# Expert stage: one row of the next turn placed ahead of a turn's ten products on the matrix engine

## The reference

```python
def peer_ffn(x, wq, subkeys, u_tab, v_tab):
    ...
        g = jax.nn.softmax(fv, axis=-1)
        a = jax.nn.gelu(jnp.einsum('thkd,td->thk', u_tab[e], xb))
        return jnp.einsum('thk,thkd->td', (g * a).astype(v_tab.dtype), v_tab[e])
...
    f = peer_ffn(x1, pwq, psk, pu, pv)
    e = jax.nn.sigmoid(x1 @ wpg) * (p @ wpp)
    return layer_norm(ALPHA * x1 + f + e, l2g, l2b)
```

## Time and profile before

| | |
|---|---|
| median of 3 runs | 4102.77 us (4099.56 to 4108.38) |
| the profiled execution | 4094.37 us, of which its span 4092.6 us |
| granted PE clock, mean of the span | 0.889 of 2.4 GHz |
| first matmul of the dense rows | 1822.9 us into the span |
| from there to the end of the span | 2269.7 us, 32 turns |
| PE, DVE, DMA engines in that part | 2000 us busy, 1422 us busy, 82, 86 and 68% in its three parts |

### The profile page before, as it was taken

How to read it: one execution, slowest core, us unless ns; L and a number is a source line. 1 busy time by engine, 2 the same in 40 slices (tenths; PEclk the granted TensorE clock), 3 DMA queues, 4 the chain that set the end, 5 groups by cost and what they waited for, 6 DMA issues and landing times.

```text
span 4092.6 us, 51077 instructions
## 1 busy us (share of the span) xinstructions
PE 3230.8 (79%) x19272; PEld 1784.5 (44%) x19272; DVE 2391.2 (58%) x4920; ACT 726.7 (18%) x1104; POOL 1113.8 (27%) x942
## 2 busy tenths in 40 slices
PE   5899773988764555526888897989987999898998
PEld 2455561444431344423444353444444454444454
DVE  3111364434379888858767666666666666664345
ACT  3111133111210222211111111111111121212111
POOL 0000000000000000005545554555454545443442
PEclk8899785999887666658899998999998999999999
DMA  6221326222300333268888887988887889887882
GB/s 188 68 75 54 115 74 228 75 85 101 136 16 6 88 88 88 83 218 282 294 282 282 286 282 262 332 315 304 311 311 265 318 321 316 297 294 268 316 305 98
DMA packets 348346, 831.39 MB, mean 203 GB/s; under 512 B 61944, under 2 KB 167328, under 8 KB 343392
## 3 DMA queue, kind: packets, MB, share of 16 engines
q0 software_dynamic: 129024, 469.82, 32.9%
q1 hardware_dynamic: 219120, 358.90, 25.7%
HBM read 741.40 MB, written 88.47 MB: 203 GB/s over the span
## 4 chain that ended last, share of the span: by engine, by line
PE 24%; DMA 13%; DVE 6%; POOL 5%; DVEq 4%; issue 3%; SPq 1%; ACT 1%; POOLq 0%; ACTq 0%
PE experts_ps L1492 11%; PE experts_ps L1478 8%; DMA experts_ut<-in_uT 7%; DMA experts_v_rows<-in_v,picks_by_choice 6%; PE experts_ps L1509 4%; POOL experts_v_rows L1597 2%; POOL experts_u_rows L1584 2%; DVEq L1696 2%; DVE experts_ul L1630 2%; DVEq L1666 1%; DVE experts_prod L1695 1%; ACT experts_uh L1536 1%; DVE experts_hl L1669 1%; DVE experts_hf L1665 1%; DVE experts_hh L1667 1%
## 5 line engine op out<-in xcount | busy, mean ns | idle before, releaser
L1584 POOL DMA_INDIRECT experts_u_rows<-in_u_rows,picks_by_token x448 | 574.2, 1282 | 786.1 <-DVEq L1696 699.0
L1478 PE MATMUL experts_ps<-experts_xh,experts_uh 128*128 128x320 f16 x2048 | 616.3, 301 | 55.2 <-DMA experts_xl<-scratch_xl 27.7
L1478 PE MATMUL experts_ps<-experts_xl,experts_uh 128*128 128x320 f16 x2048 | 615.8, 301 | 0.0
L1478 PE MATMUL experts_ps<-experts_xh,experts_ul 128*128 128x320 f16 x2048 | 615.8, 301 | 0.0
L1492 PE MATMUL experts_ps<-experts_vh,experts_hh 128*128 128x512 f16 x1280 | 502.7, 393 | 105.8 <-issue 94.7
L1695 DVE CUSTOM_DVE_ANT_0 experts_prod<-experts_u_rows,experts_x 128x1024 f16<-128x1024 f32 x448 | 545.8, 1218 | 22.6 <-issue 11.8
L1597 POOL DMA_INDIRECT experts_v_rows<-in_v,picks_by_choice x448 | 490.2, 1094 | 250.1 <-issue 125.3
L1492 PE MATMUL experts_ps<-experts_vl,experts_hh 128*128 128x512 f16 x1280 | 500.7, 391 | 0.0
L1492 PE MATMUL experts_ps<-experts_vh,experts_hl 128*128 128x512 f16 x1280 | 498.1, 389 | 0.0
L1680 DVE SCALAR_TENSOR_TENSOR experts_y<-experts_ps,experts_y 128x512 f32<-128x512 f32 x320 | 221.0, 692 | 470.7 <-PE experts_ps L1492 457.9
L1509 PE MATMUL experts_ps<-experts_v_rows,experts_sel 128*32 128x512 f32 x1792 | 271.2, 650 | 120.7 <-DMA experts_v_rows<-in_v,picks_by_choice 118.4
(11 more groups left out here) (260 smaller groups left out, 4666.9 us busy)
## 6 DMA issues: line engine op xcount, KB each, us to landing
experts_ut<-in_uT SPq DMA_DIRECT2D x128, 512.0 KB, 6.9
experts_vt<-in_v SPq DMA_DIRECT2D x128, 512.0 KB
scratch_g<-route_gbuf SPq DMA_DIRECT2D x5, 8192.0 KB, 31.2
experts_g<-scratch_g SPq DMA_DIRECT2D x128, 320.0 KB, 4.8
scratch_z<-project_z SPq DMA_DIRECT2D x10, 1984.0 KB, 7.1
project_piece<-in_w_in SPq DMA_DIRECT2D x15, 1024.0 KB
merge_w_piece<-in_w_merge SPq DMA_DIRECT2D x13, 1024.0 KB, 7.9
mix_za<-scratch_z SPq DMA_DIRECT2D x10, 960.0 KB, 4.7
```

The lines of the kernel that those rows point to most:

```text
L1478: mm = pe.matmul(ps[:, A0 + k2 % 2, 0:W], w[:, e % 2, k, :], x[:, k, c * W:(c + 1) * W], start=k == 0 and j == 0, stop=k == KT - 1 and j == 2)
L1584: pool.indirect_dma_start(u_rows[:, k % RU], None, u_table, bass.IndirectOffsetOnAxis(ap=picks.by_token[:, b, j:j + 1], axis=0)).then_inc( ...
```

## The change

The matrix engine's list gets another order: row 0 of turn i+1 now stands ahead of the ten products of turn i. Rows 1, 2 and 3 keep their place behind the products. The steps' events are attached by counting PE's own pieces of work from 0, in the new order. ACT takes the gelu of row 0 ahead of its wait for `turn_done`, and `vh` and `uh` behind it. The lists of DVE, POOL and SP are as before, and no instruction is added or removed.

```diff
@@ tensor engine @@
-                over_steps(row, expand, events)
+                step = itertools.count()
+                for i in range(TURNS + 1):
+                    if i < TURNS:
+                        first = 0
+                        row(i, first, i * ROWS + first)
+                        events(next(step))
+                    if i > 0:
+                        for q in range(2 * DB):
+                            expand(i - 1, *divmod(q, 2))
+                            events(next(step))
+                    if i < TURNS:
+                        for m in range(ROWS):
+                            if m != first:
+                                row(i, m, i * ROWS + m)
+                                events(next(step))
@@ scalar engine @@
-                def row(i, m, e):
-                    if m == 0 and i > 0:
-                        act.wait_ge(turn_done, i)
-                    act.wait_ge(v_loaded[e % 2], 16 * (e // 2 + 1))
-                    act.activation(vh[:, m], vt[:, e % 2], ACT.Copy, scale=SV).then_inc(v_high, 1)
+                def gelu(e):
                     for c in range(NC):
                         k2 = e * NC + c
                         act.wait_ge(h_temp, k2 + 1)
                         act.wait_ge(a_full, k2 + 1)
                         act.activation(act_a[:, c, :], ps[:, A0 + k2 % 2, 0:W],
                                        ACT.Gelu_apprx_tanh, scale=1.0 / SU).then_inc(a_taken, 1)
+
+                def row(i, m, e):
+                    if m == 0 and i > 0:
+                        gelu(e)
+                        act.wait_ge(turn_done, i)
+                    act.wait_ge(v_loaded[e % 2], 16 * (e // 2 + 1))
+                    act.activation(vh[:, m], vt[:, e % 2], ACT.Copy, scale=SV).then_inc(v_high, 1)
+                    if m > 0 or i == 0:
+                        gelu(e)
                     if e + 2 < KEYS:
                         high_u(e + 2)
```

More of the change, by code:

```diff
@@ L20 @@
+import itertools
 import math
```

## The result

| | before | after |
|---|---|---|
| median, 4 runs of each | 4105.3 us (4099.6 to 4108.4) | 4248.4 us (4244.1 to 4257.9) |
| the profiled execution: span | 4092.6 us | 4245.6 us |
| granted PE clock, mean of the span | 0.889 | 0.877 |

The ratio is 1.0355, with an interval of 1.0336 to 1.0375. The kernel is slower by 143 us, where the prediction had +16 and a range up to 4165. The sign was right, the size was not.

What follows compares the result with a forecast made beforehand. DVE's chain through the four rows was taken to set the first product. Terms -5, +22, -1, +1, -4, +3 and 0 summed to +16 us, 4119 us as a median; range 4080 to 4165.

Steps and rivals of the forecast that it cites:

- v events one product earlier: Turns 9 to 25, steps 9 to 13: v events lack 1.7 us of cover in 13 turns, +22 us.
- the clock: PE's half-rate stretches behind gaps in about 10 turns: taken as 0, with -17 us as the bound.
- those hanging on DVE's rows: v events waiting for DVE's rows in 11 turns: landing 2.7 us earlier, needed 2.6 earlier, -1 us.
- Row 0's gelu waits: DVE's two waits for row 0's gelu, 2.7 us a turn, go, moving DVE's later work forward.
- the first product: Turns 1 to 30: follows its `ul` by 6.6 us instead of 4.15, `ul` 2.7 earlier; -5 us in all.
- The last turn: Turn 31: PE has three rows instead of four, first product at 22 us against 26.2, -4 us.
- Rival B: Loads of `ut` do not land 2.7 us earlier: slower by more, 4220 us, half of it 4170; chance 0.11.
- Rival A: PE's gap before first products closes and stays closed: faster, some -20 to -90 us, 4013 to 4083; chance 0.21.
- Rival C: Nothing measurable: gathers run ahead, so v events cost +10 instead of +22, sum +4 us; chance 0.21.
- Batch changes: PE transposes the sparse weights three times, one product earlier, with DVE just late: 1 us each, +3 us.
- turn 0: The extra row there waits for an `ul` and ends at 1873.3 against 1872.31, +1 us.

Runs made afterwards that it cites:

- e1: The changed kernel with PE's v events kept behind the same products as before, so only the row is moved: 4068.3 us, 0.9936.
- e2: The kernel before with only PE's events of steps 4 to 13 one product earlier, row 0 not moved: 4294.2 us, 1.0481.
- e3: The changed kernel with POOL's gathers of v one step earlier in its list: 4098.8 us, 1.0004.
- e8: The changed kernel with a ring of 6 buffers instead of 5 for gathered u rows: 4117.6 us, 1.0051.
- e6: e1 with POOL's gathers of v one step earlier: 4045.9 us, 0.9859.
- e10: e1 with POOL's gathers of v two steps earlier: 4017.6 us, 0.9809.
- e4: The kernel before with POOL's gathers of v one step earlier: 4037.4 us, 0.9864.
- e11: The kernel before with gathers of v two steps earlier and a ring of 6 instead of 5 for gathered u rows: 4015.5 us, 0.9793.
- e12: The kernel before with only PE's events of steps 4 to 12 one product later: 4033.7 us, 0.9847.
- e13: The kernel before with POOL's gathers of v three steps earlier: 4023.6 us, 0.9827.

## Why the prediction was wrong in size

The sign held, and so did the mechanism named first among the losses, the v events one product earlier. The step that failed is its price: the prediction put +22 on the v events, and the runs show +172. It counted five products and one v event of cover where the trace has four and one, and it put the clock at nothing.

The event of the earlier trace rows (step 12 of turn 24) after the change, with the v event of step 8 and the dot of step 8 ahead of it:

```profile
3725.57 1.92 PE L1510 MATMUL experts_ps<-experts_v_rows,experts_sel 128*32 128x512 f32 x16 [1.94 <-DMA experts_v_rows<-in_v,picks_by_choice]
...
3730.84 1.22 DVE L1715 CUSTOM_DVE_ANT_0 experts_prod<-experts_u_rows,experts_x 128x1024 f16<-128x1024 f32 x1
...
3745.22 3.64 PE L1510 MATMUL experts_ps<-experts_v_rows,experts_sel 128*32 128x512 f32 x16 [7.26 <-DMA experts_v_rows<-in_v,picks_by_choice]
```

1. **v events one product earlier, +22, and those hanging on DVE's rows, -1.** Measured: +172 in the changed kernel (after against e1), +199 alone (e2). The step went wrong in three ways.
   - *The distance.* I counted PE's work in the earlier trace rows wrongly. Between the addition at 3595.91 and the late event lie four products and the v event of step 8, 4 x 2.6 + 1.9 = 12.3 us, not five products and a v event, 14.9. By my count it would not have had to wait, and it waited 1.50. The ring counts dots, not steps: step 9 of this turn has two dots, so the dot that frees the gather is four steps back, in step 8, where a v event stands too. One product earlier, that v event no longer lies between the dot and the late event but in front of both. Three products are left, 7.8 us against the 14.0 needed. Its wait grew from 1.50 to 7.26 us, instead of by 1.7; that of turn 14 above, which is the same case, from 1.57 to 6.40. By the kernel's plan (`sparse_plan`), 27 of the 128 v events have another v event in the step of the dot that frees their gathers: 15 in turns 2 to 8, 12 in turns 9 to 25. PE's waits in front of these 27 grew from 52 to 131 us, of a growth of 128 in all; those in front of the other 101 grew from 69 to 118. In turns 2 to 8, where steps hold more dots and where I had put -0.1 a turn, waits before v events grew from 33 to 88 us. The forecast for the whole stage was 140 to 150 against 118; it was 247.
   - *The clock.* I took 0 and a bound of -17, as if gaps could only shrink. The earlier trace rows had shown the other side already, 3.64 us for a v event behind a gap of 4.70, and I used this row only for its wait. In the traces before and after, the 24 events of 16 recorded matmuls that stand behind a wait of 3.79 us or more take 3.10 to 3.64 us, the 158 behind a wait of under 2 us take 1.92 or 1.93, and of the 10 in between some take the one and some the other. 32 v events of 128 run slowly after the change, 15 before; half-rate time grew by 119 us. The part of the loss that is slower matmuls is 48 us against e1, in PE's busy time. The Trainium skill, "TensorE: Matmul & The Clock Gate", section "Why this matters for your kernels", advises to leave no gaps above about 3 us between bursts of matmuls; the trace agrees for gaps of that length, and shows slow events behind some shorter waits too (3.52 us behind 2.58). I had weighed that advice only for the gap that closes, not for those that open.
   - *The loop.* A late v event delays the product behind it, that product's addition and dot, and with this dot the next gather. I priced the events singly. How the 144 us of new waiting divide between this and the distance isn't measured; that all of it hangs on the lead is, by e1, e3 and e8.

2. **Row 0's gelu waits and the first product, -5.** The waits went as told (`ul` of row 2 is 2.7 us earlier, 11.6 to 8.9), and the first product did not come earlier, also as told. But I had it 0.2 us earlier a turn, and it came 1.4 later in e1 and 2.3 later in the changed kernel, because it now follows its `ul` by 7.8 and 8.9 us, not by 6.6: PE still waits in front of the row, and the v event of step 4 stands ahead of the first product in the changed kernel. In turn 11 the first product was to stay near 30 us; it went from 30.2 to 33.9. PE's rows were to wait 60 us or more for `ul`; it was 41.2, and 68.8 for `a_taken`, which I had not named. Yet the row alone gave -27 (e1), more than the -5: behind the first product the turn is 2.5 us shorter (37.4 to 34.9). Of this 1.5 is PE's busy time, since the products no longer start behind a gap at half rate, and 1.0 is idle time, since v waits moved from behind the first product to in front of it. Over turns 1 to 30 e1 has 19 us less busy and 13 us less idle time than the kernel before; half-rate time falls from 195 to 126 us. So the clock term was too small on this side as well. The last turn gave -6, against -4.

3. **Rival B, the loads do not follow.** True in part and small. `ul` of row 3 and of the next row 0 came only 1.9 and 2.2 us earlier instead of 2.7, so 0.5 to 0.8 a turn, 15 to 25 us; the median landing of a load of `ut` went from 6.9 to 7.8 us, less than the 1.3 us more at which I had said that B decides. ACT's wait for these loads grew to 511.5 us, but to 490.9 in e1 too, which is faster than before. By that row alone one would have blamed the wrong thing.

4. **Rival A, faster.** It fell for the change, and e1 shows that its mechanism was there: with the v events in place, the row in front of the products gives 27 us, in part through the clock, and not through an earlier first product. **Rival C**, gathers that run ahead and soften the loss, fell.

5. **Batch changes, +3, and turn 0, +1.** PE's waits in front of the transposes grew from 0.9 to 9.7 us, so the first of these terms was about 9 us. Turn 0, from the first matmul of its rows to its tenth product, took 80.0 us before and 80.9 after, as told.

## What to carry to other kernels

Work that is moved ahead of other work on an in-order engine also moves everything that is attached to the engine's place in its list. Before pricing it, take every consumer of a prefetch in the moved stretch and count, in the unit in which its ring counts (here dots, not steps), what work is left between the release of its buffer and its use. Here the kernel already waited at that place, and the curve was steep. In such a case, put the prefetch a step earlier first, which here was worth more (-77 us for two steps) than the reordering could give (-27).

## What was not expected of the hardware

- The price of a late event lies in its wake too. The same 16 matmuls take 1.92 us behind waits of up to 1.94 us, and 3.64 us behind 4.70 and 6.40. What follows can run at half rate as well, for a short while: behind the late event of turn 14 the next four matmuls of 512 columns are recorded with 0.57 to 0.63 us and the fifth, at 3013.66, with 0.38 again.
- The two directions are unequal: one product earlier +199 us, one product later -64, two steps of lead on POOL -77 and a third nothing.
- Loads of `ut` (512 KB each) land later wherever the row is moved in front of the products, and not where the kernel is slow: the median landing is 7.6 to 9.0 us in the changed kernel, e1, e3, e6, e8 and e10, and 6.9 to 7.3 in the kernel before, e2, e4, e11, e12 and e13. e2 is the slowest with 7.0, e10 among the fastest with 9.0. The DMA engines' share fell from 0.82 to 0.77 from before to after, and gathers of v took 6.3 us in both. That the loads are bunched more closely in the rows' part of the turn may be the reason; this was not tried.
